# Newton's step on VectorE alone, q and k turned before they are scaled, and pairs of matmuls side by side on TensorE, in a two-block network on one core

## The reference

```python
def rms_norm_2(x, g):
    y = x * lax.rsqrt(jnp.mean(x * x, axis=-1, keepdims=True) + EPS)
    return y * g
# hybrid layer, rotary heads (6 block-sparse and 6 dilated; here both are masked softmaxes over 512 keys)
q = rope(rms_norm_2(to_heads(a_q), qk_g[0])); k = rope(rms_norm_2(to_heads(a_k), qk_g[1]))
p = softmax(q @ k.T * 64 ** -0.5 + mask); o = p @ v
# 4 memory heads: keys and values from 256 memory rows, no rope, no mask
y = concat(oa * silu(a_g), ob * silu(b_g), om * silu(m_g)); x = x + y @ w_out
# RWKV layer: per channel and direction
w_raw = w0 + tanh(lw) @ w2[d];  decay = exp(-exp(-softplus(-w_raw) - 0.5));  a = sigmoid(a0 + la @ a2[d])
```

## Time and profile before

| | |
|---|---|
| median of three executions | 2769.11 us (2768.67 to 2774.69) |
| profiled execution | 2775.17 us, span 2773.0 us |
| busy | PE 2362.7 us (85%), DVE 1350.5, ACT 1160.6, POOL 851.1 |
| mean granted clock of TensorE | 0.918 of full speed |

### The profile page before, as it was taken

The page is one execution under the profiler, slowest core; times in us unless marked ns, Lnnn a source line. Parts: engine busy times, 40 slices in busy tenths (PEclk is TensorE's granted clock), DMA queues, the critical chain, the costliest instruction groups (busy, mean ns, idle before and its releaser), DMA issues.

```text
span 2773.0 us, 59103 instructions
## 1 busy us (share of the span) xinstructions
PE 2362.7 (85%) x25736; PEld 1683.0 (61%) x25736; DVE 1350.5 (49%) x2266; ACT 1160.6 (42%) x1933; POOL 851.1 (31%) x562
## 2 busy tenths in 40 slices
PE   8799996589889788869788888848899988889889
PEld 2677774377667676647556655526565656555556
DVE  1368788144445454441655554533444442545452
ACT  2566665233334344322544433423444443434342
POOL 0344543100010111133443433334434334443442
PEclk9899997799989999989999998969999989899999
DMA  7134544632322222222110110011111112111111
GB/s 256 61 95 130 171 126 124 185 106 79 110 73 64 73 52 70 80 85 86 65 38 31 38 39 31 23 73 65 54 46 46 46 39 88 41 46 46 46 61 61
DMA packets 148481, 211.32 MB, mean 76 GB/s; under 512 B 81920, under 2 KB 106752, under 8 KB 147456
## 3 DMA queue, kind: packets, MB, share of 16 engines
q1 hardware_dynamic: 137120, 164.28, 19.0%
q0 software_dynamic: 9952, 40.11, 4.8%
q10 hardware_dynamic: 1152, 3.15, 0.3%
HBM read 165.30 MB, written 42.21 MB: 75 GB/s over the span
## 4 chain that ended last, share of the span: by engine, by line
PE 56%; DVE 17%; POOL 10%; issue 7%; ACT 7%; DMA 2%; SPq 0%; ACTq 0%; POOLq 0%; DVEq 0%
PE ps L258 7%; PE ps L259 6%; PE ps L260 6%; PE ps L1330 2%; POOL wbl L243 2%; PE ps L540 2%; PE ps L2710 2%; PE ps L1320 2%; PE ps L2234 2%; PE ps L1345 2%; DVE Rc L335 2%; PE ps L2732 2%; DVE p L2308 1%; POOL sqc L331 1%; POOL sqc L329 1%
## 5 line engine op out<-in xcount | busy, mean ns | idle before, releaser
L243 POOL TENSOR_TENSOR wbl<-wb,wbh 128x1024 fp32r<-128x1024 f32 x128 | 306.6, 2395 | 520.6 <-ACT wbh L238 515.8
L329 POOL TENSOR_TENSOR ro<-ro 128x256 f32<-128x256 f32 (+1 forms) x16 | 16.8, 1052 | 591.5 <-DVE ro L323 591.5
L258 PE MATMUL ps<-hT2h,wbh 128*128 128x512 f32 x416 | 185.3, 445 | 6.3 <-POOL wbl L243 4.7
L258 PE MATMUL ps<-hT1h,wbh 128*128 128x512 f32 (+1 forms) x432 | 181.7, 421 | 8.5 <-POOL hT1l L2379 4.4
L258 PE MATMUL ps<-hTh,wah 128*128 128x512 f32 (+1 forms) x512 | 178.7, 349 | 9.9 <-issue 6.4
L259 PE MATMUL ps<-hTl,wah 128*128 128x512 f32 (+1 forms) x512 | 173.3, 339 | 0.0
L260 PE MATMUL ps<-hTh,wal 128*128 128x512 f32 (+1 forms) x512 | 172.7, 337 | 0.0
L259 PE MATMUL ps<-hT2l,wbh 128*128 128x512 f32 x416 | 166.3, 400 | 0.0
L260 PE MATMUL ps<-hT2h,wbl 128*128 128x512 f32 x416 | 166.1, 399 | 0.0
L238 ACT ACTIVATE wbh<-wb 128x1024 fp32r<-128x1024 f32 x128 | 134.2, 1049 | 68.8 <-PE ps L1929 43.5
L243 POOL TENSOR_TENSOR wal<-wa,wah 128x1024 fp32r<-128x1024 f32 x34 | 108.3, 3186 | 166.8 <-ACT wah L238 166.8
(11 more groups left out here) (404 smaller groups left out, 5996.2 us busy)
## 6 DMA issues: line engine op xcount, KB each, us to landing
wb<-in_w_in SPq DMA_DIRECT2D x56, 512.0 KB, 3.4
s_str_dram<-s POOLq DMA_DIRECT2D x48, 576.0 KB, 8.7
wm<-in_ada SPq DMA_DIRECT2D x48, 512.0 KB, 4.6
bkv<-s_str_dram SPq DMA_DIRECT2D x96, 192.0 KB, 3.5
wa<-in_rw_in SPq DMA_DIRECT2D x34, 512.0 KB, 4.0
wb<-in_da_in SPq DMA_DIRECT2D x32, 512.0 KB, 3.4
ARI<-s_str_dram SPq DMA_DIRECT2D x96, 128.0 KB, 3.5
wb<-in_w_out SPq DMA_DIRECT2D x16, 512.0 KB, 3.5
```

Of the source, the lines that this page charges most:

```text
L243: e.tensor_tensor(self.lo[:, n % 2], self.raw[:, n % 3], self.hi[:, n % 2].bitcast(F32), ALU.subtract).then_inc(self.K.s.w_lo, 1)
L258: e.matmul(z, wh[:, k, :], hi[:, k, a:b], start=k == 0, stop=False)
```

## The change

- Newton's step on DVE alone in Mid, Diff, Second and the norms: `dve_first` waits for Exp instead of Ln and makes (m + n eps) r from PSUM, `dve_rest` multiplies by r/(2n) (one new pass, both inputs in SBUF) and calls `dve_last`. POOL's two products go.
- Second: ACT squares out of PSUM and then evacuates with the gain as scale. The rotation matmul needs only the evacuated q or k. sin, cos and sum come first and the product with r last; scores wait for that.
- Second: item z is query tile z // 2 and head z % 2. Scores of both heads are issued together (partitions 0-63 and 64-127, banks 4 and 5) once both banks are free. On DVE the maxima of the next two items stand ahead of `scale(z)`, on ACT both exponentials. Values of both heads are issued at the end of the pair, alternately, into the two partition halves of bank 6.
- Mix: decays and rates of both directions are issued together for 512 columns and then for 256; the second half waits for both sigmoids of the first.

```diff
+    def dve_first(self, e, i, m, M, r, eps, n):
+        e.wait_ge(self.exp, self.v0 + i + 1)
+        e.scalar_tensor_tensor(out=M, in0=m, scalar=n * eps, in1=r, op0=ALU.add, op1=ALU.mult).then_inc(self.m, 1)
+    def dve_rest(self, e, i, M, r, n):
+        e.wait_ge(self.m, self.v0 + i + 1)
+        e.scalar_tensor_tensor(out=M, in0=M, scalar=0.5 / n, in1=r, op0=ALU.mult, op1=ALU.mult).then_inc(self.p, 2)
+        self.dve_last(e, i, M, r)
...
-    def pe_decays(self, e, gp, d):
-        for j, (a, b) in enumerate(self.cols):
+    HALVES = (0, 512), (512, 768)
+    def pe_decays(self, e, gp, x):
+        s, n, (a, b) = self.K.s, 4 * gp + 2 * x, self.HALVES[x]
+        if n:
+            e.wait_ge(s.sg_sig, n)
+        for d in range(2):
+            e.matmul(self.K.psum[:, 6 + d, 0:b - a], self.lw2[64 * d:64 * d + 64, 0, 128 * gp:128 * gp + 128],
...
+        def square_evac(out, sq, use, z):
+            e.activation(sq, m, ACT.Square).then_inc(s.nr_sq, 1)
+            e.activation(out, m, ACT.Copy, scale=K.Q("qkg", 6 * (P // 8) + 2 * self.kind(P) + z, 1)).then_inc(s.evac_a, 1)
...
+        def scaled(buf, z):
+            if t:
+                e.wait_ge(s.nr_cos, o["nr_cos"] + v)
+                e.tensor_tensor(buf, buf, self.tm[z][:, :], ALU.add).then_inc(s.nr_sum, 1)
+            e.wait_ge(s.ra_r, self.ra.done(2 * P + z))
+            e.tensor_tensor(buf, buf, self.R[z][:, 0:buf.shape[-1]], ALU.mult).then_inc(s.nr_mul, 1)
...
-    def steps(self, scores, scale, finish, values):
+    def steps(self, scores, scale, finish):
         scores(0)
-        scores(1)
         yield
         for z in range(8):
+            if z % 2 == 0 and z < 6:
+                scores(z + 2)
             scale(z)
-            if z + 2 < 8:
-                scores(z + 2)
             if z:
                 finish(z - 1)
             yield
-            if z == 5:
-                values(0)
         finish(7)
         yield
-        values(1)
...
+            for j in range(2):
+                e.matmul(psum[:, 4 + j, 0:n], q[64 * j:64 * j + 64, 128 * qt:128 * qt + 128],
+                         k[64 * j:64 * j + 64, 0:n], start=True, stop=True).then_inc(s.sc_mm, 1)
```

More of the change, by code:

```diff
@@ L823, in act_post @@
         yield
[L824 to L827, removed]
+        for x, (a, b) in enumerate(self.HALVES):
+            for d in range(2):
+                e.wait_ge(s.la_mm, 4 * gp + 2 * x + d + 1)
                 K.table[0] = "sig"
-                e.activation(bd[:, a:b], K.psum[:, 4 + j, 0:b - a], ACT.Sigmoid,
+                e.activation(S9[:, 3 * d, a:b], K.psum[:, 4 + d, 0:b - a], ACT.Sigmoid,
                              bias=K.Q("a0", 8 * d + gp, 1)).then_inc(s.a_sig, 1)
[L831 to L835, removed]
+                if x == 0:
+                    continue
+                e.wait_ge(s.a_sig, 4 * gp + d + 3)
+                if gp == 0 and d == 0:
+                    e.wait_ge(s.omu_made, 3)
+                e.activation(S9[:, 3 * d + 1, :], S9[:, 3 * d, :], ACT.Identity, scale=K.Q("ka", gp, 1),
+                             bias=self.omka[:, gp:gp + 1]).then_inc(s.kd_fac, 1)
             yield
@@ L1024, in pool @@
         s = self.K.s
-        self.norm.pool_root(e)
         self.W.split_lo(e, 0)
@@ L2347, in pool_attend @@
     def pool_attend(self, e, h):
[L2348 to L2353, removed]
+        for _ in range(4):
+            yield
         if h:
@@ L2611, in dve_project, with turned @@
         q, k, sin = self.qb[b], self.kb[b], self.bc[:, 640:1152]
-        g = 6 * (P // 8) + 2 * self.kind(P)
         def rstd(z, use, w):
[L2615 to L2623, removed]
+            M, r = self.sq[z][:, 0:w], self.R[z][:, 0:w]
+            self.ra.dve_first(e, 2 * P + z, psum[:, use % 3, 0:w], M, r, 1e-6, 64.0)
+            self.ra.dve_rest(e, 2 * P + z, M, r, 64.0)
+        def turned(use, z):
             v = self.turned(P) + z + 1
@@ L2721, in finish, with values @@
             m.then_inc(s.tr_mm, 1)
[L2723 to L2725 removed]
+        def values():
+            e.wait_ge(s.tr_a, o["tr_a"] + 4 * P + 4)
+            e.wait_ge(s.tr_v, o["tr_v"] + 4 * P + 4)
             e.wait_ge(s.tok_c, o["tok_c"] + P + 1)
[L2727 removed]
+            if P:
                 e.wait_ge(s.at_y, o["at_y"] + P)
@@ L2731, in values, with exponent @@
                 q0 = 128 * y if t else 0
-                m = e.matmul(psum[64 * j:64 * j + 64, 6, q0:512], v[:, y, 64 * j:64 * j + 64],
-                             self.aT[(2 * P + j) % 3][:, y, q0:512], start=y == 0, stop=y == nk - 1,
-                             skip_group_check=True)
+                for j in range(2):
+                    m = e.matmul(psum[64 * j:64 * j + 64, 6, q0:512], v[:, y, 64 * j:64 * j + 64],
+                                 self.aT[(2 * P + j) % 3][:, y, q0:512], start=y == 0, stop=y == nk - 1,
+                                 skip_group_check=True)
             m.then_inc(s.pv_mm, 1)
-        if t:
-            e.wait_ge(s.nr_sum, o["nr_sum"] + self.turned(P) + 2)
-        else:
-            e.wait_ge(s.nr_mul, o["nr_mul"] + 2 * P + 2)
-        return self.steps(scores, lambda z: None, finish, values)
+        e.wait_ge(s.nr_mul, o["nr_mul"] + 2 * P + 2)
+        yield from self.steps(scores, lambda z: None, finish)
+        values()
     def act_attend(self, e, P):
         K, s, psum, o = self.K, self.K.s, self.K.psum, self.c0
-        def scores(z):
+        def exponent(z):
             i, n = 8 * P + z, self.keys(P, z)
```

162 lines of the change are left out of this document (65 added, 97 removed).

## The result

The changed kernel takes 2649.8 us (median of four, 2647.9 to 2656.3) against 2771.9 us for the kernel before on the same chip: a ratio of 0.956, 95% interval 0.954 to 0.959. Forecast: 2621, with 2575 to 2668 as the range. Its profiled execution has a span of 2646.1 us, 126.9 less than before.

| stretch | before | after | difference |
|---|---|---|---|
| up to Mix's first product | 82.5 | 84.1 | +1.6 |
| Mix's products | 364.1 | 360.0 | -4.0 |
| on to Mid's products (Scan, no code changed) | 767.0 | 762.4 | -4.6 |
| Mid | 116.5 | 113.6 | -2.8 |
| Diff, with its output and the next norm | 600.3 | 563.0 | -37.3 |

A forecast was written before the change was run, and what follows sets the result against it. TensorE was taken to bound the mixer and nearly the second block; differential attention idled 7.7 us a head. Terms 37.4+31.4+17.2+7+7+4+28+16 = 148 off 2775.2 gave 2627, on the median's scale 2621; range 2575 to 2668.

The forecast's parts named there:

- Newton's step and the waits that went with it: Softmax stalls in ten second-block pairs 36.2 us, differential attention 28, rotation waits 7, places with Newton alone on the path 7.
- Scores and values: Second block: both heads' matmuls overlap side by side, saving 37.4 us on scores and 31.4 us on values.
- the new stall: Second block: maxima before the scaling make TensorE wait 1.9 us in ten pairs, costing 19 us.
- new stalls equal to the old: Second block, windows with memory projections: chunks are smaller, so new stalls were set equal to old ones.
- More clock: Rival, chance 0.20: shorter stalls leave TensorE's clock up, giving back up to 30 us, for 2590.
- the fifth step: Second-block attention: fourth and fifth steps have no projection chunk between, so TensorE waits 1.9 us for scale(2).
- 38.5: Sign in the profile after: a second-block pair of heads takes near 38.5 us instead of 45.5.
- at the other places a 2.9 us chunk covers the 2.3: Second block: elsewhere in a pair, a 2.9 us projection chunk hides the 2.3 us, so no stall was priced.
- The rotations and tails: Rotations stop waiting for scaled q and k in two lone projections, 7.0 us; Newton alone at four places, together 7.
- The last pairs alone: Two pairs without projection save one set of values but lose alternating single scores: 2 us saved each, 4 together.
- Diff: Differential attention: a shorter Newton step saves 2 us at two waits a head, seven heads, 28 us; bounds 0 and 46.
- Mix: First block's mixer: decays and rates side by side save 2.0 us in each of 8 groups, 16 us; bounds 0 and 21.

The follow-up runs named there:

- Newton's step alone: The kernel before with only Newton's step on VectorE (norms, Mid, Diff, Second); 2646.9 us, ratio 0.955.
- own banks: Changed kernel with scaling before the maxima, q's product with r after the last scaling, each score matmul waiting for its bank alone; 2599.0 us, ratio 0.937.
- The scaling first: Changed kernel, but VectorE scales item z before the maxima of z+2 and z+3; 2630.4 us, ratio 0.946.
- the split ahead: Changed kernel, but in Mix GpSimd splits the next group's first weight block before its six stores; 2644.1 us, ratio 0.954.
- the turn undone: Changed kernel, but q and k are scaled by r and gain before they are turned, as before; 2671.8 us, ratio 0.962.

## Why the prediction was right, and where not

The time lies in the range and the sign is right, but 148 us were forecast for 127 between the profiled spans (122 between the medians), and two errors in the sum ran against each other. It gave 78 us to Newton's step and the waits that went with it (36.2, 28, 7 and 7) and 70 to the rest of the change. Newton's step alone brought 125 us in the stretches that it touches, and the rest brought nothing on top. That the total lies in the range is in good part luck.

**Scores and values: right in the row, not paid out in this kernel.** The rows came as forecast, and at full clock the work of a pair falls by 5.0 us (39.80 to 34.81). Yet from Newton's step alone to the whole change the fourteen pairs beside a projection grow by 4.9 us together (265.8 and 267.3 to 269.9 and 268.0), where the sum had some 69 us of gain less 19 of the new stall. With two lines of VectorE's order moved and the banks' waits parted they shrink to 246.5 and 246.6. So the work removed came off TensorE's busy time at its forecast price, the new order's waits and the clock took it in this kernel, and the best order tried got 40 us of the 69 back. Part of what is missing lies beside the memory projections, where the forecast set "new stalls equal to the old": those four pairs went from 35.5 and 33.3 us with Newton's step alone to 34.7 and 32.9 with own banks. TensorE now waits 2.7 to 2.9 us there for GpSimd's split of a weight block, which the run with Newton's step alone does not, and its clock is 0.90 for 1.00. What brings it is open, as no run takes it away. In the changed kernel the first such pair even had clock 0.86, below the 0.9 that the prediction named as a sign of being wrong; it had 0.91 before.

**Newton's step: mechanism right, term too small.** Put at 36.2 us of stalls for ten pairs, it gave 71 in the fourteen pairs beside a projection: the stalls, and the clock. "More clock" was my rival of 0.20; the run with Newton's step alone shows it (0.96 to 1.00 in a pair, 2.1 us), the changed kernel has it only in some pairs.

**The new stall: 19 us was the price of one of two places.** The wait at the fifth step was 1.87 us for 1.9. Missed were the last group (1.40 us), 0.51 us behind ScalarE's copy of v and 0.20 at the first group, together the 2.1 us by which a pair exceeds 38.5 (the sum's own terms, 45.5 less 2.73, 2.30 and 3.6 and plus 1.9, make 38.8). The step that failed is "at the other places a 2.9 us chunk covers the 2.3": the ninth and tenth steps stand next to each other as well, as the kernel's description says, and the product of q with r, put before the last scaling, is held by the weight split. I had seen that a pass over two SBUF tensors may be held, and set it to nothing since two GpSimd products go. It is 2.1 us for ten of the twelve rotary q. The Trainium skill (SBUF — State Buffer, section Who interferes with whom) says that such a pass and a GpSimd instruction that reads SBUF exclude each other for the whole instruction: 2.83 us for 0.69 agrees. The same section says that a `tensor_scalar` or a copy can contend with GpSimd too: the scaling's 2.41 us for 0.49 agrees.

**The rotations and tails.** The two projections that run alone fell by 11.4 us. The waits of 7.0 us for the scaled q and k went, but not for my reason: they are also absent with Newton's step alone, where q and k are still scaled first and the two projections take 68.3 us.

**The last pairs alone** were to gain 2 us each and lost 0.2: without the alternation of single scores, TensorE waits for two exponentials before a group of scores, 3.16 us at the first. The scaling first brings the 22.3 us of such a pair to 20.5, own banks to 20.3. With the old order of scores and values side by side (the values added to Newton's step alone) it takes 20.2, so the forecast's gain of values was there and the new order took it.

**Diff**: -28 forecast, -37.3 measured, with some 3.6 of the tails in it. Waits for L2305 fell from 45.6 to 17.1 us, 28.5, as forecast. 12.4 us came back as idle time before the values for which the profile names no cause (5.5 before, 17.9 now), and TensorE's busy time fell by 16 us (491.2 in 588.0 us at clock 0.89; 474.8 in 553.0 at 0.94).

**Mix** was to give 16 us and gave 4. The matmul rows are as forecast (512 columns of both directions 1.06 us from start to start), but "here TensorE is the bound, so it is paid out in full" failed: 42.7 busy of 43.5 us left 0.8 us of cover, and a chain through the other engines holds the group. In the changed kernel the groups between the first and the last take 41.7 to 44.6 us, 43.5 in the mean for 43.7 before; 3 of the 4 us come from the first and the last. With the split ahead they take 43.2 each, with the new rates or the old. Which loop sets that is open: the split behind the stores, the sigmoid's wait and the bonus each took the place of the other.

**Mid** fell by 2.8 us, with Newton's step alone as well. The forecast had 1.8 for the norm at its end; Mid's readout norm, which starts on VectorE 18 us after Mid's first products and is changed in the same way, was missing from the sum. No run takes the two apart.

## What to carry to other kernels

A stall removed from a nearly saturated TensorE is worth its own length and the clock that it costs the work around it; a term for each belongs in the sum. Work removed from it is paid out only until the next engine's chain sets the pace (5.0 us of work less gave 3.7 in a pair here). So for each place where two steps stand together write down what was between them: here two moved lines were worth 49 us, and values moved out of a gap cost more than their halving gave. When a pass over SBUF moves, look up which weight split stands beside its new place before it gets a price of nothing.

## What the runs showed of the hardware

- The granted clock of a pair took one of two values for nearly the same waits: in the changed kernel 39.00 us at 1.00 and 40.60 at 0.96 with the same instructions, 1.6 us apart in span and in busy time. With the turn undone, a pair with longer waits (40.4 us, busy 35.18) had 1.00. Total idle time doesn't predict it.
- Column halves of the array that write one bank overlap: 16 matmuls of two heads in 2.37 us, 8 of one in 2.37. In turn they take 3.93, less than twice one head.
- A scaling with one SBUF tensor input took 2.41 us for 0.49 beside a weight split; a product of two 2.83 for 0.69.
